# A chunked recurrence with the halves of its inverse crossed over the array's quarters, and spare expert rows cleared under the projection

## The reference

```python
xn = rms_norm(x)
proj = concat([x_prev, xn]) @ w_in                     # r, k, v of the RWKV-7 heads; q, k, v of attention
# RWKV-7, 8 heads of 64, for every token t:
sa = einsum('bhvk,bhk->bhv', s, -kk_t)
s  = s * w_t + sa[..., None] * (kk_t * a_t) + v_t[..., None] * k_t
y  = einsum('bhvk,bhk->bhv', s, r_t)
h  = x + concat([group_norm(y) ..., dilated_attention(q, k, v)]) @ w_out
h  = h + moe(rms_norm(h))                              # 32 experts, two for each token
```

## Time and profile before

| | us |
|---|---|
| median of 3 runs | 3348.49 (3344.24 to 3349.88) |
| the profiled execution | 3340.29 |
| its span | 3338.5 |
| projection, from the span's start to | 943.7 |
| recurrence, to about | 1523 |
| TensorE busy in the span | 3077.3 (92%) |
| VectorE, ScalarE, GpSimd busy | 1315.1 (39%), 1001.3 (30%), 318.5 (10%) |

### The profile page before, as it was taken

One profiled execution on the slowest core, in us unless ns is written; L12 is line 12 of the kernel. 1 busy time (PEld: TensorE's weight loads), 2 busy tenths in 40 slices (PEclk: granted clock), 3 DMA queues, 4 the chain that ended last, 5 costly groups with the idle time before them and its releaser, 6 DMA issues. The chain is left out here.

```text
span 3338.5 us, 74902 instructions
## 1 busy us (share of the span) xinstructions
PE 3077.3 (92%) x31005; PEld 2103.6 (63%) x31006; DVE 1315.1 (39%) x3233; ACT 1001.3 (30%) x2127; POOL 318.5 (10%) x353
## 2 busy tenths in 40 slices
PE   6999999999989889998999969997999999999990
PEld 4677666766668888887877835554555555555540
DVE  3454345544334434435766556653111111111117
ACT  3345323543222222225654633330111111111112
POOL 0000000000010000112333000000100001000004
PEclk9999999999989999998999989997999999999995
DMA  6121112111233343226767675416768777686558
GB/s 216 65 70 54 57 48 73 67 48 42 77 143 117 109 150 124 79 87 193 212 203 196 123 247 157 149 37 249 246 233 281 253 270 243 229 286 241 208 195 316
DMA packets 284771, 533.54 MB, mean 160 GB/s; under 512 B 94578, under 2 KB 108786, under 8 KB 278372
## 3 DMA queue, kind: packets, MB, share of 16 engines
q1 hardware_dynamic: 238604, 390.43, 34.8%
q10 hardware_dynamic: 25128, 66.26, 6.3%
q0 software_dynamic: 20784, 73.15, 6.1%
HBM read 394.99 MB, written 134.79 MB: 159 GB/s over the span
## 5 line engine op out<-in xcount | busy, mean ns | idle before, releaser
L287 PE MATMUL proj_main_ps<-proj_xt,proj_w 128*128 128x257 f32 x1536 | 349.6, 379 | 0.0
L287 PEld LDWEIGHTS proj_main_ps<-proj_xt,proj_w 128*128 128x128 f32 x1536 | 288.6, 190 | 41.0
L2687 PE MATMUL moe_y_ps<-moe_w,moe_ht 128*64 128x512 f32 x1312 | 301.1, 601 | 3.2 <-ACT moe_ht L2726 3.2
L2444 PE MATMUL out_proj_ps<-out_w,out_ct 128*128 128x512 f32 x544 | 241.7, 597 | 6.0 <-DMA out_w<-in_w_out_dram 6.0
L352 PE MATMUL proj_main_ps<-proj_w,proj_xt 128*128 128x512 f32 x512 | 225.3, 593 | 0.0
L2737 ACT ACTIVATE moe_sg<-moe_gate 128x256 f32<-128x256 f32 x82 | 31.6, 385 | 538.7 <-PE moe_gate L2671 538.7
L2687 PEld LDWEIGHTS moe_y_ps<-moe_w,moe_ht 128*64 128x64 f32 x1312 | 87.3, 137 | 158.7 <-issue 155.3
L2773 DVE COPY moe_y<-moe_y_ps 128x512 f32<-128x512 f32 x82 | 56.7, 692 | 313.9 <-PE moe_y_ps L2687 313.9
L2444 PEld LDWEIGHTS out_proj_ps<-out_w,out_ct 128*128 128x128 f32 x544 | 101.6, 192 | 121.9 <-issue 121.1
L1316 DVE COPY_PREDICATED rwkv_t<-ahead_rwkv_cons,rwkv_level_ps 128x512 f32<-128x512 uint32 (+1 forms) x168 | 109.8, 664 | 173.0 <-PE rwkv_level_ps L1031 173.0
L352 PEld LDWEIGHTS proj_main_ps<-proj_w,proj_xt 128*128 128x128 f32 x512 | 97.0, 190 | 108.6 <-issue 107.1
(11 more groups left out here) (405 smaller groups left out, 5455.7 us busy)
## 6 DMA issues: line engine op xcount, KB each, us to landing
moe_w<-in_expert_w_dram SPq DMA_DIRECT2D x64, 2048.0 KB, 8.9
y_rows<-rwkv_zero POOLq DMA_DIRECT2D x65, 512.0 KB, 5.0
kept_first_gate<-in_expert_w_dram SPq DMA_DIRECT2D x16, 2048.0 KB, 9.7
kept_first_up<-in_expert_w_dram SPq DMA_DIRECT2D x16, 2048.0 KB, 15.1
y_rows<-moe_y ACTq DMA_DIRECT2D x164, 128.0 KB, 6.1
ft_p<-proj_uf SPq DMA_DIRECT2D x32, 642.0 KB, 3.2
rwkv_feat<-ft_p SPq DMA_DIRECT2D x12, 1284.0 KB, 6.9
att_s_k<-in_cache_att_k_dram ACTq DMA_DIRECT2D x14, 1024.0 KB, 7.3
```

What stands on the lines that cost most here:

```text
L287: last = mm(out[:, 0:w + 1], W[:, k, kind * C + m * P:kind * C + (m + 1) * P], XT[n % 2][:, k, 0:w + 1], start=(k == 0), stop=(k == KT - 1))
L2444: last = mm(proj_ps[j][:], CT[t % 2][:, k, :], W[:, k, 512 * j:512 * (j + 1)], start=(k == 0), stop=(k == KT - 1))
L2687: last = mm(py[j * HB:(j + 1) * HB, :], HT[:, c, r * HB:(r + 1) * HB], W2[s][:, k, j * 512:(j + 1) * 512], start=(k == 0), stop=(k == FE / ...
```

## The change

Five edits in the recurrence and one that reaches from the recurrence to the projection:

1. The second half of `T` moves to the other sub-chunk's partitions, and so do `W`, one of the five row tensors of `U` and the `values` product. `w` now writes to the other half of the columns. The first half of `grow` (line 1028) uses the two quarters off the diagonal, the second (1031) the two on it, by turns. `hg` and `values` use the two off the diagonal.
2. The two groups of four heads become one of eight: one wait, one copy of 128x512 on ScalarE and one predicated copy of 128x1024 on VectorE for each level. `level_ps` is one tensor of two banks: bank 0 takes `w` and line 1028, bank 1 takes line 1031.
3. In a level 3 and 4, VectorE does both masked copies of the chunk ahead before the `put`, no longer one before each half of it.
4. On TensorE `n_products` moves ahead of `w(i, 5)`, and `values` between `w(i, 5)` and `grow(i, 5)`; ScalarE copies the values before `y`.
5. Two copies become two halves each, since they cross the partitions: `rows` for j = 0 on ScalarE, and the last copy of `begin` on VectorE.
6. The zeros: only rows from 4096 of `y_rows` on are cleared (33 stores in place of 65), by GpSimd in the projection, 5 or 6 after each of the first six `carried` copies. The zero tile is a part of `next_F[0]`, so SP waits for the stores before it loads the first features.

```diff
@@ projection, GpSimd
+            nc.gpsimd.memset(zero, 0.0).then_inc(zero_set, 1)
+            g.wait_ge(zero_set, 1)
             for n in range(1, NP):
                 g.wait_ge(xt_copied, copies_before(n))
...
                 nc.gpsimd.tensor_copy(XT[n % 2][:, :, 0:1], XT[(n - 1) % 2][:, :, CW:CW + 1]).then_inc(carried, 1)
+                for j in range(ZB * (n - 1) // (NP - 2), min(ZB, ZB * n // (NP - 2))):
+                    rows = spare_rows[j * P:(j + 1) * P, :]
+                    g.dma_start(rows, zero[0:rows.shape[0]]).then_inc(zeros_stored, 16)
+            g.wait_ge(zeros_stored, 16 * ZB)
@@ rwkv_chunks, GpSimd
-                for j in range(ZB * n // NT, ZB * (n + 1) // NT):
-                    g.dma_start(zero_rows[j * P:(j + 1) * P, :], zero[:]).then_inc(zeros_stored, 16)
@@ TensorE
             def w(i, l):
-                for g in range(2):
-                    pe.wait_ge(t0, 3 * i + 3)
-                    if base(i) + l > 1:
-                        pe.wait_ge(t_set[g], base(i) + l - 1)
-                    for hh in range(4):
-                        h = 4 * g + hh
-                        for c in range(2):
-                            last = mm(level_ps[g][part(c), hh * DH:(hh + 1) * DH], NB[i % 3][part(c), h, 0:DH], T[i % 3][part(c), h, 0:DH],
-                                      start=True, stop=True, skip_group_check=True)
-                    last.then_inc(w_done[g], 1)
+                pe.wait_ge(t0, 3 * i + 3)
+                if base(i) + l > 1:
+                    pe.wait_ge(t_set, base(i) + l - 1)
+                for h in range(H):
+                    for c in range(2):
+                        last = mm(level_ps[other(c), 0, h, :], NB[i % 3][part(c), h, 0:DH], T[i % 3][part(c), h, 0:DH],
+                                  start=True, stop=True, skip_group_check=True)
+                last.then_inc(w_done, 1)
 
             def grow(i, l):
...
+                pe.wait_ge(w_copied, base(i) + l)
+                for h in range(H):
+                    for c in range(2):
+                        if l < levels_of(i):
+                            mm(level_ps[part(c), 0, h, :], T[i % 3][other(c), h, DH:P], W[other(c), h, :],
+                               start=True, stop=True, skip_group_check=True)
+                    for c in range(2):
+                        last = mm(level_ps[other(c), 1, h, :], W[other(c), h, :], T[i % 3][other(c), h, DH:P],
+                                  start=True, stop=True, skip_group_check=True)
+                last.then_inc(g_done, 1)
...
+                if head:
+                    n_products(i + 1)
                 if longer:
                     w(i, 5)
                 if head:
-                    n_products(i + 1)
+                    values(i + 1)
                 if longer:
                     grow(i, 5)
                 if tail:
                     step(i - 1, 1)
-                if head:
-                    values(i + 1)
@@ ScalarE
             def w_copy(i, l):
-                for g in range(2):
-                    a.wait_ge(w_done[g], base(i) + l)
-                    nc.scalar.copy(W[g][:].rearrange("p h k -> p (h k)"), level_ps[g][:, 0:4 * DH]).then_inc(w_copied[g], 1)
+                a.wait_ge(w_done, base(i) + l)
+                nc.scalar.copy(W[:], level_ps[:, 0]).then_inc(w_copied, 1)
@@ VectorE
-            def put(i, l, g):
-                v.wait_ge(g_done[g], base(i) + l)
...
+            def put(i, l):
+                v.wait_ge(g_done, base(i) + l)
+                x0 = 0 if l < levels_of(i) else 1
+                halves = T[i % 3][:].rearrange("p h (x k) -> p x h k", x=2)[:, x0:2]
+                block = level(l).rearrange("p (x o k) -> p x o k", x=2, o=1)[:, x0:2].broadcast_to([P, 2 - x0, H, DH])
+                v.copy_predicated(halves, block.bitcast(U32), level_ps[:, x0:2]).then_inc(t_set, 1)
```

More of the change, by code:

```diff
@@ L81, in projection @@
         O = sb("o", [P, C])
+        zero = next_F[0].rearrange("p m k -> p (m k)")[:, 0:D]
+        ZB = -(-spare_rows.shape[0] // P)
         x_ps, ag_ps, c_ps = ps("x_ps"), ps("ag_ps"), ps("c_ps")
@@ L905, in rwkv_chunks @@
         NAT, SI, SO, SN = ring("nat", [P, C], 2), ring("si", [P, 4, 2, DH], 2), ring("so", [P, 4, 2, DH], 2), ring("sn", [P, C], 2)
-        head_ps, level_ps, tail_ps, state_ps = ([ps(f"{n}_ps{j}") for j in range(2)] for n in ("head", "level", "tail", "state"))
+        head_ps, tail_ps, state_ps = ([ps(f"{n}_ps{j}") for j in range(2)] for n in ("head", "tail", "state"))
+        level_ps = ctx.enter_context(nc.psum_tensor("rwkv_level_ps", [P, 2, H, DH], F32))
         f_cleared, f_spread = sem("sample_tiles_cleared"), sem("sample_tiles_spread")
@@ L925, in rwkv_chunks @@
         part = lambda c: slice(c * DH, (c + 1) * DH)
+        other = lambda c: part(1 - c)
         by_parity = lambda x: x.rearrange("p (q e) k -> p e q k", e=2)
@@ L1082, in values @@
                     for c in range(2):
-                        last = mm(head_ps[0][part(c), h * DH:(h + 1) * DH], KK[n % 3][part(c), h, 0:DH], U[n % 3][part(c), 3, h, :],
+                        last = mm(head_ps[0][other(c), h * DH:(h + 1) * DH], KK[n % 3][part(c), h, 0:DH], U[n % 3][part(c), 3, h, :],
                                   start=True, stop=True, skip_group_check=True)
@@ L1095, in hg @@
                         for c in range(2):
-                            last = mm(tail_ps[g][part(c), hh * P:(hh + 1) * P], T[n % 3][part(c), h, DH:P], U[n % 3][part(c), 0:5:4, h, :],
+                            last = mm(tail_ps[g][part(c), hh * P:(hh + 1) * P], T[n % 3][other(c), h, DH:P], U[n % 3][other(c), 0:5:4, h, :],
                                       start=True, stop=True, skip_group_check=True)
@@ L1251, in rows @@
                     a.wait_ge(turned, 4 * n + j + 1)
-                    nc.scalar.copy(U[n % 3][:, j].rearrange("p h k -> p (h k)"), head_ps[b][:]).then_inc(u_copied, 1)
+                    if j == 0:
+                        for c in range(2):
+                            last = nc.scalar.copy(U[n % 3][other(c), j].rearrange("p h k -> p (h k)"), head_ps[b][part(c), :])
+                    else:
+                        last = nc.scalar.copy(U[n % 3][:, j].rearrange("p h k -> p (h k)"), head_ps[b][:])
+                    last.then_inc(u_copied, 1)
             def hg_copy(n):
@@ L1326, in begin @@
                     v.copy_predicated(by_parity(T[n % 3][:])[:, e, :, 0:DH], wide(level(0)[:, 0:DH], 4).bitcast(U32), four(head_ps[e][:, 0:256])).then_inc(t0, 1)
-                v.copy_predicated(T[n % 3][:, :, DH:P], wide(level(0)[:, DH:P], H).bitcast(U32), NB[n % 3][:, :, 0:DH]).then_inc(t0, 1)
+                for c in range(2):
+                    block = level(0)[part(c), DH:P].rearrange("p (o k) -> p o k", o=1).broadcast_to([DH, H, DH])
+                    last = v.copy_predicated(T[n % 3][other(c), :, DH:P], block.bitcast(U32), NB[n % 3][part(c), :, 0:DH])
+                last.then_inc(t0, 1)
             def parts(n):
@@ L1351, in _ @@
                 if levels:
[L1352 to L1353 removed]
+                    put(i, 1)
                 if longer:
[L1355 to L1356 removed]
+                    put(i, 2)
                 if tail:
@@ L1379, in _ @@
                 if longer:
-                    put(i, 5, 0)
-                    put(i, 5, 1)
+                    put(i, 5)
                 if tail:
```

62 lines of the change are left out of this document (17 added, 45 removed).

## The result

| | median us (lowest to highest) | ratio to before, 95% interval |
|---|---|---|
| before | 3346.36 (3331.15 to 3356.17) | |
| after | 3316.11 (3304.46 to 3331.27) | 0.9927 (0.9906 to 0.9948) |
| after, a second time, on another chip | 3319.90 (3311.09 to 3327.22) | 0.9918 (0.9893 to 0.9943) |

The change takes some 27 to 30 us by the medians. The ratio is estimated from all runs of both kernels and is not the quotient of the two medians; by it the change takes 24 us (18 to 32) on the first chip and 27 on the second. The forecast was 3317.5.

A forecast was written before the change was run, and what follows sets the result against it. The prediction took the arrival of TensorE's instruction blocks to bound the recurrence. Zeros -30, crossed grow -11, start +7, outside the window -4 and clock +7 gave -31 us: 3348.5 to 3317.5 us, range 3290 to 3342.

The forecast's parts named there:

- What bounds the kernel: Recurrence: instruction blocks for TensorE cost at least some 3.5 us each, whatever their matmuls cost, and aren't fetched far ahead.
- the 89 us "above the floor": Recurrence, 1010 to 1456 us: time beyond 102 blocks at 3.5 us (357 us), split among feature loads, zeros and the rest.
- Zeros, -30 in the window and -5 outside: Recurrence: removing zero stores saves 2.0 us for each of 15 bursts from 1010 to 1456 us, and 5 us outside.
- Crossed grow, -11: Recurrence, grow at levels 1 to 4: the four-quarter pace gains 11 us, between bounds of 0 and 56.
- The half of 22 us: Recurrence: share taken as the crossed grow's gain, from 22 us of blocks that TensorE itself makes longer than 3.5 us.
- One group, 0 to +1: Recurrence: one group of eight heads costs nothing while the next block is missing, and +1 us for chunk 1.
- Clock, +7: Recurrence: quicker grow lengthens stops behind feature loads to 2 us; six more half-clock spells cost 7 us (0 to 20).
- Start, +7: Projection start: the first five zero stores delay the third token tile by 7 us, between bounds of 0 and 7.0.
- Rival 1: Recurrence: the instruction fetch doesn't bind; crossed grow gives 60 us, zeros nothing, the start costs 7: 3295 us; chance 0.17.
- Rival 2: Recurrence: the crossing gives nothing, grow keeps 0.029 us a record, and only the zeros count: 3330 us; chance 0.12.
- Rival 3: Recurrence: slower by the clock, with 48 half-clock spells in place of 6, about 3370 us; chance 0.10.
- Rival 4: Gain and loss cancel: zeros cost 1.2 us a burst (-18), crossing nothing, start and clock +14: 3345 us; chance 0.08.

The follow-up runs named there:

- repeated grow: The changed kernel with grow at level 2 of each of 16 chunks done nine times over, on four quarters: 3558.06 us, ratio 1.0658.
- Crossing alone: The changed kernel with the 65 zero stores back in the recurrence and none under the projection: 3332.07 us, ratio 0.9969.
- zeros alone: The kernel before, with only the zero stores changed: 65 leave the recurrence, 33 come under the projection: 3322.29 us, ratio 0.9927.
- zeros later: The changed kernel with the first zero burst behind the second token-tail copy instead of the first: 3309.84 us (ratio 0.9908), then 3318.64 (0.9901).
- no feature loads: The changed kernel without the recurrence's twelve feature loads; chunks 4 to 15 use the first four chunks' features: 3263.19 us, ratio 0.9778.
- grow nine times on two quarters: The changed kernel with its matmuls back on the two diagonal quarters and grow at level 2 done nine times over: 3564.77 us, ratio 1.0679.
- uncrossed: The changed kernel with the crossed matmuls back on the two diagonal quarters, keeping one group of eight and the moved zeros: 3330.55 us, ratio 0.9955.

## Why the prediction was right

- **What bounds the kernel.** Right, and shown: in the repeated grow a block of instructions costs 3.7 to 3.8 us however fast the matmuls in it are, one block more in an ordinary chunk 3.1 to 3.6, and every longer stop without a named releaser stands at the end of a block. The floor of "some 3.5 us" was low by 0.25, the lower end of the distances in place of their mean. Over 102 blocks that is 26 us: of the 89 us "above the floor" only some 60 were there to be explained, and for this reason a chunk without a load takes 26.7 us and not 24 to 25.
- **Zeros, -30 in the window and -5 outside.** The sign and the place were right, the size was not: the recurrence lost 21.6 us where I had 35, and the part in the window is near the lower bound (18). 1.3 us a burst is what the one chunk shown had (1.2). I took 2.0 by "a block waits for half a burst", which no row had shown; the nearest row was the better guide.
- **Crossed grow, -11.** Right by the recurrence: 8.8 us by undoing it, 10.6 by doing it alone. Four-quarter grow is there, and the fetch takes the rest. The half of 22 us that I took had no row behind it; that it came out is in part luck.
- **One group, 0 to +1.** Nothing in the recurrence speaks against it (-1.4, inside the scatter); the timed medians leave it open. The put was forecast at 1.35 us and takes 1.33.
- **Clock, +7.** Wrong in sign: 7 us at half clock in place of 20 (7 to 10 in the four profiles of this recurrence). The step that failed adds six new spells behind the feature loads to the six of before. "Crossing alone" shows that half of it held (41 us at half clock with the zeros in place); but the old spells didn't stay: with the zeros gone and no crossing ("zeros alone") 10 of the 20 us at half clock are left. I had taken the clock under each part, not under the two together. "It decides at a stop of 2.0 us" was too simple as well: after has a spell behind a stop of 1.89 us and none behind one of 2.23.
- **Start, +7.** 5.3 us by this pair of profiles, 6 by the means of nine with the stores at 20 us (942.2) and five without (936.1) (44.64 where I wrote 46; the recurrence begins at 949.2 and ends at 1492.0, where I wrote 951 and 1492); "zeros later" takes it back.
- **Sum.** Zeros -22, group -1, crossing -9, start +5: -27 where I had -31; what the clock gave back is inside the first and third of these. The errors, 13 us too much for the zeros and 7 too much for the clock, stood against each other, and without that luck the forecast would not have come within 2 us of the median. The measured 24 to 30 us agree with the sum; the single profile has -23, since its attention was 6 us longer.
- **Rival 1** (3295) falls with the packets and with both kinds of grow repeated. **Rival 2** falls with the eight records in 0.11 us. By the Trainium skill (TensorEngine Tiling (Array Packing), Gotcha 1: PSUM Pressure) different row tiles can't access one bank at the same time; here w's crossed halves write into one bank at 0.029 us a record, no slower than before. **Rival 3** needed 48 spells; there are two or three in the four profiles of this recurrence. It is what the crossing would have moved towards without part 6. **Rival 4** was nearest in its price of a burst, but the crossing did give something; its 3345 also leaves out the -4 outside the window and should have been some 3340.
- The Trainium skill's "mostly hidden" (Runtime: NRT & Kernel Launch, Instruction fetch mechanics) does not hold for these matmuls: 1.65 to 1.93 us of every 3.8 stand open in the repeated grow.

The distance isn't the transfer: packets take a share of the engines that is near 2%. The 2.5 us from packet to record are shorter than it, so they don't set it by themselves either; the 1.2 us from the record to the next packet are the rest of it. What those two times are spent on is open.

## What to carry to other kernels

Before making small matmuls quicker, count the instruction packets of the stretch and multiply by their distance where nothing else runs (here 3.8 us for 128 matmul records): if the stretch is about that long, a quicker array hardly pays, and more instructions cost their blocks; that fewer would pay follows, but wasn't run. The sign of it is that stops named "issue" stand at one place modulo 256 of TensorE's records. In such a stretch the large transfers were on the path though nothing waited for them by name: move them to a stretch whose blocks last long, but not to where a load is already awaited. Splitting the loads into four didn't help here.

## What the runs showed of the hardware

- Blocks of 16 KB for TensorE came 3.7 to 3.9 us apart in the mean of each profile where no large transfer ran, never nearer than 3.2 us, also at a DMA share of 0.02 and with TensorE idle for 43% of the time. A block's packet started 1.04 us or more after TensorE had got into the block before, and its first record came 2.2 to 2.9 us after the packet.
- Loads and stores delay them: 1.3 us for a burst of 1.7 MB of zeros (48 x 0.52 / 15), 1.4 to 1.7 us net for 1.3 MB of features, and the same bytes cost the same in one transfer and in four.
- TensorE's granted clock fell to 0.50 (1.2 GHz) at long stops, 1.76 us the shortest that I found at a spell, and never in the window in the three kernels whose longest stops there were 1.61 to 1.79 us (no feature loads, grow nine times on two quarters, uncrossed). The length of the stop doesn't decide alone: one of 2.23 us (the row above at 1137.60) and those of 1.93 in the repeated grow left the clock at 1.00; one of 4.59 us went with 6.8 us at half clock, but so did one of 2.23 in after's second profile, and one of 4.07 us before went with 3.4. The stretch behind the stop of 2.23 us, with the clock in the third column from the end:

```profile
1137.60:1141.00 3.40, 2.27 (x127) 2.13 (x127) 1.41 (x4) 0.00 (x0) 0.00 (x0) 1.00 0.02 5
```

- 64 x 64 matmuls in f32 on all four quarters run at 0.0146 us a record against 0.029 on two; here one half of them wrote to one bank and the other to a second.
